# The boundaries between the stages of a two-block transformer kernel: residual update, norm and first projections rewritten slice by slice

## The reference

```python
h = x
h = h + 0.5 * rmsnorm(swiglu(rmsnorm(h, ffn1_pre_g), w1g, w1u, w1d), ffn1_post_g)     # stage 1
u = rmsnorm(h, mix_pre_g)                                                             # stage 2
y_ssd, y_att = ssd_branch(u @ w_in[...]), diff_attn_branch(u @ w_in[...])
h = h + rmsnorm((gates(u)[0] * y_ssd + gates(u)[1] * y_att) @ w_out, mix_post_g)
h = h + 0.5 * rmsnorm(swiglu(rmsnorm(h, ffn2_pre_g), w2g, w2u, w2d), ffn2_post_g)
u = rmsnorm(h, norm1_g)                                                               # stage 3
h = h + (gates(u)[0] * gated_delta_rule(u) + gates(u)[1] * sparse_attention(u)) @ w_out2
u = rmsnorm(h, norm2_g)                                                               # last FFN
gate, val = split(causal_conv3(u @ ffn_w_up) + ffn_conv_b)
h = h + (silu(gate) * val) @ ffn_w_down
out = rmsnorm(h, final_g)
```

## Time and profile before

| | |
|---|---|
| median of 3 executions | 2868.2 us (2863.16 to 2868.34) |
| the profiled execution | 2860.19 us, span 2858.4 us |
| mean granted TensorE clock | 0.962 of full speed |
| busy: PE matmul, weight load | 92%, 72% |
| busy: DVE, ACT, POOL | 53%, 39%, 4% |
| DMA | 209.93 MB, 73 GB/s |

### The profile page before, as it was taken

How to read it: one execution, slowest core, us unless ns; L and a number is a source line. 1 busy time by engine, 2 the same in 40 slices (tenths; PEclk the granted TensorE clock), 3 DMA queues, 4 the chain that set the end, 5 groups by cost and what they waited for, 6 DMA issues and landing times. The chain is left out here.

```text
span 2858.4 us, 33690 instructions
## 1 busy us (share of the span) xinstructions
PE 2618.0 (92%) x13778; PEld 2044.9 (72%) x13778; DVE 1500.9 (53%) x2280; ACT 1125.3 (39%) x1687; POOL 125.9 (4%) x98
## 2 busy tenths in 40 slices
PE   8999978998998999988999978988898997899998
PEld 6888846766776776767888846756667675688886
DVE  5444266656566664345443254587644445466632
ACT  4222234555544455443222234242424255344422
POOL 0000020000000000010000020000000000100000
PEclk9999989999999999999999988999999998999999
DMA  4333312221221221222233311111111110233332
GB/s 139 97 102 91 101 52 69 67 68 58 82 72 47 74 67 59 82 81 74 96 96 98 94 54 59 53 52 38 52 38 45 60 59 23 74 96 96 98 99 76
DMA packets 59193, 209.93 MB, mean 73 GB/s; under 512 B 6560, under 2 KB 6560, under 8 KB 59040
## 3 DMA queue, kind: packets, MB, share of 16 engines
q1 hardware_dynamic: 57600, 204.38, 22.8%
q10 hardware_dynamic: 1440, 3.41, 0.3%
HBM read 205.66 MB, written 2.10 MB: 73 GB/s over the span
## 5 line engine op out<-in xcount | busy, mean ns | idle before, releaser
L1349 PE MATMUL bank<-uR,hl 128*128 128x512 f32 x2232 | 923.2, 414 | 54.5 <-DVE uR L1962 27.1
L1350 PE MATMUL bank<-uR,hl 128*128 128x512 f32 x2232 | 885.6, 397 | 0.0
L1351 PE MATMUL bank<-uR,hl 128*128 128x512 f32 x2232 | 884.5, 396 | 0.0
L1950 DVE TENSOR_TENSOR hl<-raw,hl 128x1024 fp32r<-128x1024 f32 (+1 forms) x391 | 473.1, 1210 | 618.1 <-ACT hl L1668 617.3
L1349 PEld LDWEIGHTS bank<-uR,hl 128*128 128x128 f32 x2232 | 429.0, 192 | 189.9 <-issue 67.5
L1668 ACT CAST hl<-raw 128x1024 fp32r<-128x1024 f32 (+1 forms) x391 | 402.4, 1029 | 249.4 <-PE bank L1351 248.3
L1351 PEld LDWEIGHTS bank<-uR,hl 128*128 128x128 f32 x2232 | 428.2, 192 | 93.7
L1350 PEld LDWEIGHTS bank<-uR,hl 128*128 128x128 f32 x2232 | 429.2, 192 | 85.9 <-issue 5.2
L1349 PE MATMUL bank<-act,hl 128*128 128x512 f32 x528 | 205.4, 389 | 0.0
L1350 PE MATMUL bank<-act,hl 128*128 128x512 f32 x528 | 205.4, 389 | 0.0
L1351 PE MATMUL bank<-act,hl 128*128 128x512 f32 x528 | 205.4, 389 | 0.0
(11 more groups left out here) (434 smaller groups left out, 2595.3 us busy)
## 6 DMA issues: line engine op xcount, KB each, us to landing
raw<-in_win SPq DMA_DIRECT2D x147, 512.0 KB, 3.5
raw<-in_w SPq DMA_DIRECT2D x44, 512.0 KB, 3.5
raw<-in_w1g SPq DMA_DIRECT2D x22, 512.0 KB, 3.5
raw<-in_w1u SPq DMA_DIRECT2D x22, 512.0 KB, 3.5
raw<-in_w2g SPq DMA_DIRECT2D x22, 512.0 KB, 3.5
raw<-in_w2u SPq DMA_DIRECT2D x22, 512.0 KB, 3.5
raw<-in_w1d SPq DMA_DIRECT2D x16, 512.0 KB, 3.5
raw<-in_wssd SPq DMA_DIRECT2D x16, 512.0 KB, 3.6
```

The costliest lines, as they stand in the source:

```text
L1349: e.matmul(s.bank[:, :], h[:, 0, w], hi, start=s.first and q == 0, stop=False)
L1350: e.matmul(s.bank[:, :], h[:, 0, w], lo, start=False, stop=False)
L1351: i = e.matmul(s.bank[:, :], h[:, 1, w], hi, start=False, stop=s.last and q == n - 1)
L1950: e.tensor_tensor(h[:, 1, 0:s.width], x[:, 0:s.width], h[:, 0, 0:s.width].bitcast(F), ALU.subtract).then_inc(*sig("dve_split.lo", s))
```

## The change

At boundaries 1, 2 and 3 one step, `boundary`, takes the place of `post_norm` and of the pre-norm. The sum matmul over the first seven columns is issued ahead of the stage's last matmuls, the last column's squares go straight into the same bank, the last column itself is read from its bank. `step("warm")` loads the table of Ln and Exp ahead of the last projection. Then each slice is multiplied, added to hT, rounded and squared on ACT and its low half made on DVE, before the next slice's; and three panels of the next stage (`lead`) take each slice together, in three banks. The squares are added in a tree on DVE, the root follows within the fourth panel, and the results of the first panels are multiplied by it (`scale`). Where the next stage is a mixer (`normed`), six panels are taken so, u is then normalized as before (`norm_x`, `norm_u`), and the consumers of the six find them in `ahead`, without matmuls or yields of their own. At boundary 2 four panels are taken so. At boundary 4 `fold_h` rounds, squares and splits each column's slice as it is added, and the last FFN is scaled late in all of its 44 panels (`late.update`). GpSimd's parts of `collect`, `post`, `sumsq` and `norm` are gone. The con load's DMA is issued on ACT's queue behind the root. Cut to its core:

```diff
     def ugemm(src):
+        if id(src) in ahead:
+            return ahead.pop(id(src))
         b = MB.take()
         j = panel(src, KB * 128)
...
-            c.t = [("dve_col.add" if m == KB - 1 else "pool_col.add", s)]
+            c.t = [("dve_col.add", s)]
...
+    def boundary(ys, b7, b_sum, gpost, half, gpre, srcs, normed, drop=None, con=None):
+        q = fp.take()
+        s = step("last_sq", b=b7, q=q)
+        js = [panel(srcs[0], KB * 128)]
+        r = rstd([(q[:, :], [("act_col.sq", s)])], O1024, b_sum)
+        if con is not None:
+            con()
...
+        s = step("post_fold", ys=ys, b=b7, r=r, gpost=gpost, half=half, gpre=gpre, h=[list(t) for t in t_h],
+                 hr=[list(t) for t in t_hr], last=list(u_last), qs=qs)
...
+        js += [panel(src, KB * 128, False) for src in srcs[1:3]]
+        for part in range(2):
+            s2 = step("sq_sum", s=s, qs=qs, part=part, before=s2 if part else None)
...
+            open_split(js[0] + NHL + part)
...
+        bs = [MB.take(), MB.take(), SB.take()]
+        s = step("lead", js=js, bs=bs, s=s)
...
+        for n, src in enumerate(srcs[3:]):
+            j = panel(src, KB * 128)
+            b = (SB, SB, MB)[n].take()
+            for q in range(0, KB, STEP):
+                if n == 0 and q == KB // 2:
+                    r = late["r"] = rstd([(acc[:, :], acc.t)], O1024, r=fp.take_of(low))
...
+                b.t = [mm(j, b, [u_at(k) for k in range(q, q + STEP)], q == 0, q + STEP == KB, off=q)]
...
+            if n == 0:
...
+                for i in range(3):
+                    ahead[id(srcs[i])] = scaled(bs[i], r)
+                if normed:
+                    xs = [fp.take() for _ in range(KB)]
+                    s_x = step("norm_x", g=gpre, r=r, xs=xs, h=[list(t) for t in t_h])
...
+            if n:
+                ahead[id(srcs[n + 2])] = scaled(bs[n + 2], r)
...
+            s = step("norm_u", xs=xs, s=s_x, last=last)
...
+        ahead[id(srcs[-1])] = scaled(b, r)
...
+    boundary(ys, b7, b_sum, "ffn1_post", True, "mix_pre", [WIN[j] for j in (80, 16, 17, 18, 19, 32)], True,
+             con=lambda: step("con", c=0, after=t_phase))
...
+    boundary(ys, b, b_sum, "mix_post", False, "ffn2_pre", [G2[0], U2[0], G2[1], U2[1]], False,
+             drop=lambda: t_all.extend(drop_pages(NB1, rp, 1)))
...
+    boundary(ys, b7, b_sum, "ffn2_post", True, "norm1", [W2[j] for j in (32, 0, 8, 16, 1, 9)], True,
+             con=lambda: step("con", c=1, after=t_phase))
...
         b.release(*t_h[m])
+        fold_h(m, "norm2", qs, KB)
...
+    late.update(acc=qs[0], r=None)
...
+        def lead(s):
...
+            for k in range(KB):
+                w = slice(k * 128, (k + 1) * 128)
+                go.wait_ge(*on("act_norm.hi", s.s, k))
+                if k < KB - 1:
+                    for b, h in zip(s.bs, hs):
+                        e.matmul(b[:, :], h[:, 0, w], uR[:, 0, k, :], start=k == 0, stop=False)
+                    for b, h in zip(s.bs, hs):
+                        e.matmul(b[:, :], h[:, 1, w], uR[:, 0, k, :], start=False, stop=False)
+                    go.wait_ge(*on("dve_norm.lo", s.s, k))
+                    for b, h in zip(s.bs, hs):
+                        e.matmul(b[:, :], h[:, 0, w], uR[:, 1, k, :], start=False, stop=False)
...
+        def post_fold(s):
...
+            mul(0)
+            add(0)
+            mul(1)
+            lo(0)
+            add(1)
+            for k in range(2, KB):
+                mul(k)
+                add(k)
+                lo(k - 1)
+            lo(KB - 1)
```

More of the change, by code:

```diff
@@ L272, in build @@
     late = {}
+    ahead = {}
     stream = {"n": 0}
@@ L279, in build, with open_split, panel @@
     step("setup", s=s_init)
-    def panel(src, width):
+    def open_split(j):
+        splits[j] = step("split", j=j, width=0)
+    def panel(src, width, next_split=True):
         j = stream["n"]
@@ L285, in panel @@
         splits[j]["width"] = width
-        splits[j + NHL - 1] = step("split", j=j + NHL - 1, width=0)
+        if next_split:
+            open_split(j + NHL - 1)
         return j
@@ L295, in u_at, with scaled @@
         return uR[:, 0, k, :], uR[:, 1, k, :], t_u[k]
+    def scaled(b, r):
+        x = fp.take()
+        s = step("scale", b=b, r=r, x=x)
+        x.t = late["t"] = [("dve_norm.scaled", s)]
+        b.release(*x.t)
+        return x
     def ugemm(src):
+        if id(src) in ahead:
+            return ahead.pop(id(src))
         b = MB.take()
@@ L309, in ugemm, with rstd @@
                 c.release(("pe_norm.sum", late["r"].s))
[L310 to L315, removed]
-        return b
-    def rstd(src, which):
-        b, r = SB.take(), fp.take()
-        s = step("rstd", src=src, which=which, b=b, r=r)
+            return scaled(b, late["r"])
+        return b
+    def rstd(src, which, b=None, r=None):
+        first = b is None
+        b, r = b or SB.take(), r or fp.take()
+        s = step("rstd", src=src, which=which, b=b, r=r, first=first)
         b.release(("act_norm.ln", s))
@@ L363, in norm_late @@
         late.update(acc=acc, r=None)
[L365 to L387, removed]
     def end_u():
@@ L404, in collect, with sum_first @@
         else:
-            c.t = [("dve_col.add" if m == KB - 1 else "pool_col.add", s)]
+            c.t = [("dve_col.add", s)]
             q.release(*c.t)
         ys.append(y)
[L409 to L413, removed]
+    def sum_first(c):
+        b = SB.take()
+        s = step("sum_first", c=c, b=b)
+        c.release(("pe_norm.first", s))
+        return b
@@ new lines, in boundary, with fold_h @@
+        u_last[:] = b.t
+        if normed:
+            s = step("norm_u", xs=xs, s=s_x, last=last)
+            for k in range(KB):
+                t_u[k] = [("dve_norm.lo", s, k)]
+                t_hr[k] = [("dve_norm.x", s_x, k)]
+                xs[k].release(*t_u[k])
+        ahead[id(srcs[-1])] = scaled(b, r)
+        if normed:
+            r.release(*late["t"])
+            late.clear()
+    def fold_h(m, gname, qs, stage):
+        q = fp.take_of(low) if m == 0 else fp.take()
+        c = q if m == 0 else qs[0]
+        s = step("fold_h", m=m, g=gname, h=list(t_h[m]), last=list(u_last), q=q, c=c, ct=list(c.t),
+                 add=0 < m < stage)
+        if m == 0:
+            q.t = [("act_norm.sq", s)]
+        elif m < stage:
+            c.t = [("dve_norm.add", s)]
+            q.release(*c.t)
+        else:
+            q.t = [("act_norm.sq", s)]
+        qs.append(q)
+        if gname:
+            t_u[m] = [("dve_norm.lo", s)]
```

297 lines of the change are left out of this document (172 added, 125 removed).

## The result

The changed kernel takes **2871.8 us** (median; 2868.5 to 2874.1), the one before, run beside it on the same chip, 2863.2 (2860.2 to 2868.3): ratio 1.0028, 95% interval 1.002 to 1.0036. It is slower by 8.6 us. The forecast was slower, at 2882, with a range of 2842 to 2897. The profiled execution has a span of 2871.2 us against 2858.4, 12.8 more; the forecast's sum, made against that span, was +14.2.

What follows compares the result with a forecast made beforehand. PE bounds the last FFN; ACT and DVE in lock step are the mixers' chain. Boundary terms -14.4+3.4+9.1+17.4-1.3 give +14.2 us, on the median 2868.2 a forecast of 2882; range 2842 to 2897.

Steps and rivals of the forecast that it cites:

- Root and lead: At the boundaries: DVE's first multiply at T0+3.6 instead of 5.6, PE's first next-stage matmul at T0+5.9; T0 starts the last main matmul.
- Boundary 2: Stage 2 to FFN 2, already scaled late: four panels end at 32.7 us against 47.0, a gain of 14.4 us.
- Boundary 1: Into stage 2, a mixer: the 22 us lead is lost to norm and serial convs; +2.5 us, +0.86 for the sum.
- Boundary 3: Into stage 3, a mixer: the burst again, and side work dealt out later; +9.1 us with the sum matmul.
- the delta rule's late start: Stage 3: first squares at T0+104 where before has T0+88.5; +3.2 us for work done meanwhile, +5 for hold turns.
- hold turns: Stage 3: main stream holds some 16 turns longer for the delta rule, about 22 us, PE idling 23%: +5 us.
- Boundary 4: Into the last FFN: 17.6 us gained at once, but scales make the in-order chain 12.59 us a pair; in all +17.4 us.
- Boundary 5: The kernel's end: root 2.1 us shorter, sum matmul 0.86 us, together a gain of 1.3 us.
- A: Rival: the last FFN's chain doesn't bind since PE's panels queue ahead; sum -20.8, 2847 us; chance 0.14.
- D: Rival: each last-FFN pair's surplus is half as large, the boundary before it gives 0; sum -3.2, 2865 us; chance 0.06.
- B: Rival: the lead into both mixers is kept, -22.4 us each, 2825; half kept, 2847; chance 0.12 together.
- C: Rival: delta rule's late start alone sets stage 3, and repeated last-FFN idle lowers the clock; +35, 2903 us; chance 0.1.

## Why the prediction was right or wrong

The direction was right, and so was the main mechanism, the chain of the last FFN. The size was not: beside the 2863.2 us of the kernel before, 2882 is 18.8 more, and 8.6 were measured. The step that failed is the term of boundary 3.

**Root and lead: right.** First multiply at T0+3.6 (forecast 3.6), first matmul at T0+5.9 (5.9).

**Boundary 2: right.** -14.4, measured -14.6 in the traces; from boundary 2 to 3 the two kernels with the old boundary take 384.3 us, the fourteen with the new one 369.6 to 370.5 (this stretch repeats far better than the mixers).

**Boundary 1: right in kind.** The norm's end at T0+46.7 (forecast 47), first silu 429.1 (429.6), ninth panel's split 454.2 (454.5), sixth silu 463.4 (463.7), PE's wait at the decay 422.7 to 437.5 (421 to 438). The forecast's times were on the clock of the trace before, whose T0 is 1.1 us earlier, so from T0 on these rows came 0.3 to 1.6 us sooner than forecast. The price, +3.4 with the sum, measured +2.5 in one pair of traces and +1.7 between the means of six kernels with the new boundary (902.3) and three with the old (900.6); the runs bound boundaries 1 and 3 together to 2 to 4 us.

**Boundary 3: the step that failed.** The landmarks held (last silu of the burst T0+82.8 for 82, first squares T0+107 for 104). The term was oversized: 8.2 us of it were the delta rule's late start, 3.2 for work done meanwhile and 5 for hold turns. The 3.2 does not come from the figures beside it: squares 15.5 us later, with 18.3 us of work done by then that was not, would be a gain of 2.8. In this kernel that start is worth 1.5 us (the run with four yields). I had priced the main stream's turns by PE's idle share, as if the delta rule alone set the pace there; ACT and DVE's serial chain set it. Only when that was cut did the same start weigh 9.9 us: it is the next bound, not a term that adds to the first. Against the forecast's 8.2 the stretch measured +3.6 in the pair of traces and about +1.2 over five kernels with the new boundary (mean 808.7) against three with the old (807.4).

**Boundary 4: right in mechanism, 4 us short.** The chain was forecast at 12.59 us a pair and is 12.64; over 21 pairs that makes 1.1 us. The rest is behind the last pair, 19.3 us from its scale to the first column for my 16.4:

```profile
2743.71 0.62 ACT L1841 CAST act<-fA 128x512 fp32r<-128x512 f32 x1 [2.33 <-DVE fA L2175]
2744.35 1.28 ACT L1805 ACT_TABLE_LOAD   x1
2745.65 2.73 ACT L1774 CAST hl<-raw 128x768 fp32r<-128x768 f32 x3
```

I had counted `warm`'s table load only as a gain at the root. Here it stands ahead of the down projection's splits, for which PE waits: 1.3 us of the 2.9. The rest is TensorE's clock. PE waited 1.87 us for the low half, and from about 1 us behind that wait nine matmuls took 3.6 us where they take 2.0 at the full clock:

```profile
2747.59 0.50 PE L1433 MATMUL bank<-act,hl 128*128 128x512 f32 x1 [1.87 <-DVE hl L2070]
```

```profile
2750.00:2752.00 2.00, 2.00 (x7) 1.51 (x6) 0.00 (x0) 0.00 (x0) 0.00 (x0) 0.50 0.82 237
```

In the run with the split behind the scale PE waits for nothing there, and neither cost is paid. Two cuts at the chain (split behind scale, silu behind split) and one removal (no late scale) each brought the pair back to 10.88.

**Boundary 5: right**, -2.2 and +0.9.

**The base.** Of the 10 us between 2882 and 2871.8, 5 are the median of before: 2868.2 in three executions, 2863.2 in fourteen. Of the other 5.6 (14.2 forecast, 8.6 measured) the two traces show 1.4: the forecast had 4.6 too much at boundary 3 and 0.9 at boundary 1, and 4.0 too little at boundary 4. That these errors nearly cancel is luck. The other 4.2 are scatter: the profiled execution of the kernel before lay 3.0 us below its median, that of the changed one 1.2 above. A sum made against one execution can't see this.

**The rivals.** A and D (the chain of the last FFN hides) fall with its 12.64 us. B (the lead is kept) falls with the three kernels that put boundaries 1 and 3 back. C had two parts: the delta rule's start as the sole bound, refuted above, and the clock. PE waited 36 times in the 240 us shown, 0.6 us each and at most 1.0, and the granted clock of that window is 1.00. Still each wait cost about 0.3 us more than its length: a pair takes 1.76 us longer than 10.88, while its two waits are 0.2 and 0.95 us. The profile counts a matmul as busy for 0.39 us though the next one starts 0.23 us behind it, and the first behind a wait (2708.74) is 0.34 us ahead of the next; so PE's busy share is 91% there where the forecast, counting matmuls, had 87. The Trainium skill warns of waits that repeat ("TensorE: Matmul & The Clock Gate", HAM oscillation). Waits of 0.6 us did not bring the half clock back; one of 1.87 us, right behind four of 0.2 to 0.95, was followed by it for some 3 us, once, where C had five restarts. Behind the wait of 14.8 us the clock is lower too: 0.76 in the 30 us that begin with its end, which hold the wait of 5.6 us as well, where before has 0.94.

**What the forecast did not see.** I read the mixers' lock step as 5.15 us a panel against 5.44 and so as nearly hidden. That compared ACT and DVE's projection work with PE's projection work alone and left out that each of the three also has side work in its list. That the chain falls back behind this side work again and again is my reading and was not tested by itself; what the runs show is that shortening the chain is worth 38 us in the kernel before.

## What to carry to other kernels

Where two in-order engines hand each other short steps, count the latency of the round trip, not the busy shares: DVE at 64% and ACT at 38% of the window bound the last FFN. Then look for one independent instruction to put into each wait (a split between scale and taps, a rounding between tap and silu); such an edit of a few lines was worth 38 us twice, with no work removed.

A lead made at a boundary is worth only what the next bound lets through. Before building it, cut the chain behind it, and check how the side work is dealt out: with yields tied to computed panels, panels taken ahead starve it.

## What was not expected of the hardware

A table load cost little more than its row: in all bursts the next activation starts 1.29 to 1.30 us after a load begins (441.17 to 442.47 in the run with silus behind taps). The load itself starts when the row ahead has ended (429.12 + 0.63, 429.76), where an activation would start 0.1 us sooner (442.53, 443.06). The drain that the Trainium skill adds ("ScalarE: Activation LUTs", What ACT_TABLE_LOAD costs) appears in no row here.

The whole stretch of 30 us in which PE did nothing behind boundary 3 has a mean granted clock of 0.58:

```profile
1703.00:1733.00 30.00, 0.00 (x0) 0.00 (x0) 18.66 (x28) 14.38 (x20) 0.00 (x0) 0.58 0.06 18
```

A window with no matmul in it is thus not at 0.50 throughout: the granted clock was 1.00 from 1703 to 1707, 0.66 in the next 2 us and 0.50 from 1709 on. In the last FFN thirty-six waits of 20.8 us in all, none over 1.0, left it at 1.00, and one of 1.87 us behind the last pair did not.
